# 512 weight columns per product, instead of 256, in the value and Fourier projections of a fused two-block kernel

## The reference

```python
for l in range(DEPTH):                       # DEPTH = 2
    proj = h @ w_in[l]                       # 1024 -> 2048: q, k, v, u of 512 columns each
    a = diff_attention(q, k, v, lam, ...)    # 8 heads, two softmaxes per head, minus each other
    f = fourier_mix(u, w_f[l], b_f[l])       # FFT over features and tokens of u, then a product
    h = layer_norm(ALPHA * h + concat(a, f) @ w_o[l])
    h = layer_norm(ALPHA * h + swiglu(h))
# second block: swiglu, then a mixer whose one input projection holds q, k, v, gates and a
# short convolution (stick-breaking attention, 8 heads), then swiglu
```

## Time and profile before

| | |
|---|---|
| median of 3 runs | 1327.15 us (1324.51 to 1329.25) |
| span of the profiled execution | 1327.0 us |
| PE busy | 1239.0 us, 93% |
| PE weight loads busy | 1183.8 us, 89% |
| DVE busy | 857.9 us, 65% |
| ACT busy | 589.8 us, 44% |
| mean granted clock | 0.964 |

### The profile page before, as it was taken

The page is one execution under the profiler, slowest core; times in us unless marked ns, Lnnn a source line. Parts: engine busy times, 40 slices in busy tenths (PEclk is TensorE's granted clock), DMA queues, the critical chain, the costliest instruction groups (busy, mean ns, idle before and its releaser), DMA issues.

```text
span 1327.0 us, 23836 instructions
## 1 busy us (share of the span) xinstructions
PE 1239.0 (93%) x9572; PEld 1183.8 (89%) x9572; DVE 857.9 (65%) x1077; ACT 589.8 (44%) x693; POOL 14.1 (1%) x30
## 2 busy tenths in 40 slices
PE   4998799999999988999994999999999997999996
PEld 3886699999897687999994999999998997999996
DVE  7674756777857657577778467778458567544445
ACT  5543444333444335344335433444487534444432
POOL 0000000000000000000000000000000000000000
PEclk9999899999899898999996999998999998999998
DMA  7510256677442113577770467773432553455540
GB/s 285 201 64 32 96 191 231 270 276 282 175 149 86 63 64 129 188 284 276 271 275 33 174 224 283 283 274 140 154 133 96 191 188 130 160 190 190 184 164 32
DMA packets 34093, 235.95 MB, mean 178 GB/s; under 512 B 3600, under 2 KB 7200, under 8 KB 7408
## 3 DMA queue, kind: packets, MB, share of 16 engines
q1 hardware_dynamic: 28960, 196.10, 40.2%
q0 software_dynamic: 3584, 38.22, 7.8%
q10 hardware_dynamic: 1488, 0.76, 0.2%
HBM read 234.02 MB, written 1.05 MB: 177 GB/s over the span
## 4 chain that ended last, share of the span: by engine, by line
PE 86%; DVE 6%; ACT 4%; issue 3%; DMA 1%; SPq 0%; DVEq 0%; ACTq 0%
PE bank L335 78%; PE bank L454 2%; ACT w_hi L670 2%; PE bank L434 1%; PE bank L474 1%; DVE rstd L967 1%; PE bank L486 1%; DMA raw<-stream 1%; DVE partial L1011 1%; PE bank L466 1%; DVE w_lo L937 1%; DVE state L960 1%; PE bank L450 0%; DVE state L973 0%; DVE x_lo L979 0%
## 5 line engine op out<-in xcount | busy, mean ns | idle before, releaser
L937 DVE TENSOR_TENSOR w_lo<-raw,w_hi 128x2048 fp32r<-128x2048 f32 x184 | 421.4, 2290 | 240.9 <-ACT w_hi L670 238.3
L335 PE MATMUL bank<-x_hi,w_hi 128*128 128x256 f32 x1888 | 541.3, 287 | 25.3 <-DVE x_lo L979 24.3
L335 PE MATMUL bank<-x_lo,w_hi 128*128 128x256 f32 x1888 | 537.9, 285 | 0.0
L335 PE MATMUL bank<-x_hi,w_lo 128*128 128x256 f32 x1888 | 537.5, 285 | 0.0
L670 ACT ACTIVATE w_hi<-raw 128x2048 fp32r<-128x2048 f32 x184 | 350.2, 1906 | 156.9 <-PE bank L335 154.3
L335 PEld LDWEIGHTS bank<-x_hi,w_hi 128*128 128x128 f32 x1888 | 366.0, 194 | 32.0 <-DVE x_lo L979 15.8
L335 PEld LDWEIGHTS bank<-x_lo,w_hi 128*128 128x128 f32 x1888 | 366.2, 194 | 0.0
L335 PEld LDWEIGHTS bank<-x_hi,w_lo 128*128 128x128 f32 x1888 | 366.0, 194 | 0.0
L335 PE MATMUL bank<-hid_hi,w_lo 128*128 128x256 f32 x704 | 197.9, 281 | 0.0
L335 PE MATMUL bank<-hid_hi,w_hi 128*128 128x256 f32 x704 | 197.3, 280 | 0.0
L335 PE MATMUL bank<-hid_lo,w_hi 128*128 128x256 f32 x704 | 195.8, 278 | 0.0
(11 more groups left out here) (158 smaller groups left out, 1175.7 us busy)
## 6 DMA issues: line engine op xcount, KB each, us to landing
raw<-stream SPq DMA_DIRECT2D x184, 1024.0 KB, 4.8
work<-ada POOLq DMA_DIRECT2D x24, 1536.0 KB, 7.1
state<-xT SPq DMA_DIRECT2D x4, 256.0 KB, 3.6
outT<-state SPq DMA_DIRECT2D x4, 256.0 KB, 2.2
c<-consts SPq DMA_DIRECT2D x1, 960.0 KB, 9.9
wf<-w_f ACTq DMA_DIRECT2D x2, 256.0 KB, 3.1
c<-consts POOLq DMA_DIRECT2D x1, 384.0 KB, 5.6
lp<-layer_params ACTq DMA_DIRECT2D x2, 83.5 KB, 2.5
```

What stands on the lines that cost most here:

```text
L335: last = nc.tensor.matmul(out, stationary, moving, start=start and i == 0, stop=stop and i == 2, skip_group_check=True)
L937: nc.vector.tensor_tensor(w_lo[j % SLOTS][:, :], raw[j % SLOTS][:, :], w_hi[j % SLOTS][:, :].bitcast(F32), ALU.subtract).then_inc(lo_ready, 1)
```

## The change

A chunk of v or u now holds 4 tiles of input features for all 512 output columns, where it held 8 tiles for 256; the stream is repacked on the host and keeps its size and its count of chunks. `token_projection` replaces the natural products: for each tile and each half of the tokens three products that stream 512 columns into a whole bank. Bank 0 gets tokens 0 to 127 and bank 1 the others, and both are complete only when the second of the two chunks is through. So PE's count of natural products goes from 480 to 240, with the same number of streamed columns.

```diff
+            def token_projection(t, j, banks, xh, xl, c, before=lambda k: None):
+                pe.wait_ge(lo_ready, 3 * t + (j + 1))
+                wh, wl = chunk(w_hi, j % SLOTS, 4), chunk(w_lo, j % SLOTS, 4)
+                for i in range(4):
+                    k = 4 * c + i
+                    before(k)
+                    for m in range(2):
+                        cols = slice(m * P, (m + 1) * P)
+                        last = passes(banks[m][:, :], wh[:, i, :], wl[:, i, :], xh[:, k, cols], xl[:, k, cols], True,
+                                      k == 0, k == KT - 1)
+                last.then_inc(chunk_done, 1)
...
-                projection_pair(t, V0, B[0:2], x_hi, x_lo, lambda k: pe.wait_ge(x_ready, 16 * l + (k + 1)),
-                                natural=True)
+                for c in range(2):
+                    token_projection(t, V0 + c, B[0:2], x_hi, x_lo, c, lambda k: pe.wait_ge(x_ready, 16 * l + (k + 1)))
...
                     if s >= 2:
                         transpose_a(s - 2)
-                    if s % 2 == 0:
-                        pe.wait_ge(proj_evac, 8 * l + (j - 1))
-                    projection(t, j, B[j % 2], x_hi, x_lo, ks=range(4 * (s % 2), 4 * (s % 2) + 4),
-                               natural=j in (U0, U1))
+                    if s < 4:
+                        if s % 2 == 0:
+                            pe.wait_ge(proj_evac, 8 * l + (j - 1))
+                        projection(t, j, B[j % 2], x_hi, x_lo, ks=range(4 * (s % 2), 4 * (s % 2) + 4))
+                    elif s % 2 == 0:
+                        if s == 4:
+                            pe.wait_ge(proj_evac, 8 * l + 6)
+                        token_projection(t, j, B[0:2], x_hi, x_lo, j - U0)
...
+                def evacuate_tokens(j, out):
+                    act.wait_ge(chunk_done, 3 * t + (j + 2))
+                    for m in range(2):
+                        nc.scalar.activation(out[:, m, :], B[m][:, :], ACT.Copy).then_inc(proj_evac, 1)
...
                 split(t, 2, first=True)
-                evacuate(V0)
+                split(t, 3)
+                evacuate_tokens(V0, v_s)
+                split(t, 4)
...
-                    if s < 8 and s % 2 == 1:
+                    if s in (1, 3):
                         evacuate(Q1 + s // 2)
+                    elif s == 5:
+                        split(t, U0 + 3)
+                    elif s == 7:
+                        evacuate_tokens(U0, u_s)
+                        split(t, U1 + 3)
...
-            projection_pair(t, 0, B[0:2], x_hi, x_lo, input_tile(6), natural=True)
+            for c in range(2):
+                token_projection(t, c, B[0:2], x_hi, x_lo, c, input_tile(6))
```

More of the change, by code:

```diff
@@ L529, in _ @@
                         pe.wait_ge(consts_landed, 32)
-                    if s == 4:
-                        pe.wait_ge(proj_evac, 8 * l + 6)
                     scores(s)
@@ L754, in evacuate @@
                     act.wait_ge(chunk_done, 3 * t + (j + 1))
[L755 to L762, removed]
+                    half = 0 if j in (Q0, K0) else 1
+                    nc.scalar.activation((qT if j in (Q0, Q1) else kT)[:, 2 * half:2 * half + 2, :],
+                                         B[j % 2][:, :].rearrange("p (m n) -> p m n", m=2), ACT.Copy,
+                                         scale=HD ** -0.5 if j in (Q0, Q1) else 1.0).then_inc(proj_evac, 1)
                     split(t, j + 3)
+                def evacuate_tokens(j, out):
+                    act.wait_ge(chunk_done, 3 * t + (j + 2))
+                    for m in range(2):
+                        nc.scalar.activation(out[:, m, :], B[m][:, :], ACT.Copy).then_inc(proj_evac, 1)
                 def exps(h):
@@ L796, in _ @@
                    .then_inc(wf_landed, 16)
-                for j in (V1, Q0, K0):
+                for j in (Q0, K0):
                     evacuate(j)
@@ L853, in _ @@
                 if j < 2:
-                    out, scale = v_s[:, :, j * S:(j + 1) * S], 1.0
-                elif j % 2 == 0:
+                    if j == 1:
+                        for m in range(2):
+                            nc.scalar.activation(v_s[:, m, :], B[m][:, :], ACT.Copy).then_inc(proj_evac, 1)
+                    split(t, j + 3)
+                    continue
+                if j % 2 == 0:
                     out, scale = qT[:, j - 2:j, :], VD ** -0.5
@@ L1455 @@
         w_in = _tiles(a["w_in"][l], KT, 256)
-        q, k, v, u = w_in[0:2], w_in[2:4], w_in[4:6], w_in[6:8]
+        q, k = w_in[0:2], w_in[2:4]
+        v, u = _tiles(a["w_in"][l][:, 2 * ATT:3 * ATT], 4, ATT), _tiles(a["w_in"][l][:, 3 * ATT:], 4, ATT)
         chunks += [v[0], v[1], q[0], k[0], q[1], k[1], u[0], u[1]]
@@ L1461 @@
     m = _tiles(a["w_mix_in_2"][0], KT, 256)
-    cb, cc, cx, q, k, v, ga, gb = m[0:2], m[2:4], m[4:6], m[6:8], m[8:10], m[10:12], m[12:16], m[16:20]
+    cb, cc, cx, q, k, ga, gb = m[0:2], m[2:4], m[4:6], m[6:8], m[8:10], m[12:16], m[16:20]
+    v = _tiles(a["w_mix_in_2"][0][:, 5 * ATT:6 * ATT], 4, ATT)
     chunks += [v[0], v[1], q[0], k[0], q[1], k[1], *cb, *cc, *cx, *ga, *gb]
```

## The result

Four runs of the changed kernel gave 1343.9 us in the median (1343.48 to 1345.86), four of the kernel before 1326.16 us (1324.51 to 1329.25). The ratio is 1.0135 with a 95% interval of 1.0117 to 1.0152: 18 us slower. The forecast was 1338 us with an upper end of 1344: the side is right and the size too small. The median lies 0.1 us under that end; the ratio on the 1327.15 us that the forecast started from gives 1345.1, 1 us over it.

What follows compares the result with a forecast made beforehand. PE, busy 93% of the span, was taken as the bound, with DVE and ACT close behind in the head stages. Value projections 0.7, bunching 5.8 and clock 4.5 gave +11.0 us on 1327.0: 1338 us, range 1328 to 1344.

Steps and rivals of the forecast that it cites:

- Wide product: On PE at full clock, a product of 512 columns takes 0.2267 us, between bounds of 0.2133 and 0.24.
- Hand-over: From last value product to Q0: 1.15 us start to start, as ACT waits for both banks; 0.72 us more, three times.
- The value side as a whole: Three value projections: 1.5 us saved in products, 2.2 us lost before Q0, net +0.7 us (-0.7 to +2.2).
- Bunching at full clock: Head stages: whole U0 and U1 delay scores of heads 4 and 6; 2.9 us longer a layer, 5.8 in all.
- Clock, first stretch: Head stages, 80.44 to 89.87 in layer 0: the clock falls, costing 1.5 to 4.9 us, middle 3 a layer.
- if it falls: Clock term of the head stages: +4.5 us in sum, between 0 and +8.3 should the clock fall, -1.5 otherwise.
- Clock, what goes away: Layer 1 head stages: the old clock fall, paid at 439.20, is replaced, -1.5 us.
- Clock, second stretch: From 95.31 to past 104 in layer 0: the clock falls, but last scores have 2.5 us of slack; nothing counted.
- A: Head stages: only the bunching counts and the clock falls no more than before, 1332 to 1333.5 us; chance 0.18.
- B: PE alone decides: later scores are caught up by slack, fewer products save 5.4 us, 1324 us; chance 0.1.
- C: Whole kernel: saving and bunching cancel within measurement, 1327 to 1331 us; chance 0.12.
- D: Clock falls in both stretches of a layer, the second also reaching the last head, 1341 to 1345 us; chance 0.1.

Runs made afterwards that it cites:

- 5 full products: Changed kernel plus 5 zero-operand products of 512 columns on all 128 rows in stage 5: 1336.45 us against 1327.35 for the kernel before, ratio 1.0071.
- U halved: Changed kernel with each wide chunk of U0 and U1 cut in two, over stages 4 to 7: 1328.21 us against 1328.74 for the kernel before, ratio 0.9993.
- the narrow bunched one: Kernel before, 256 columns wide, with all of U0 in stage 4 and all of U1 in stage 6: 1344.37 us against 1328.74, ratio 1.0114.
- the one with only U1 cut: Changed kernel with U0 whole in stage 4, U1 cut in two over stages 6 and 7: 1340.84 us against 1327.35 for the kernel before, ratio 1.0105.
- the one with 32 rows: Changed kernel plus 5 zero-operand products on 32 of 128 rows in stage 5: 1344.34 us against 1326.46 for the kernel before, ratio 1.0130.

## Why the prediction fell short

The mechanism and the places were right. The step that failed is the size of one term, what the fallen clock costs in the first stretch; two smaller terms of the clock were off as well and cancel each other.

- Wide product: 0.2267 us estimated, 0.2273 measured.
- Hand-over: 1.15 us estimated, 1.15 measured. The value side as a whole was put at +0.7 us. It is +1.5 in the profile, of which 0.75 is left with the clock evened out, and +2.1 (0.9 to 3.3) when made alone.
- Bunching at full clock: 2.9 us a layer estimated, 2.95 measured (with 5 full products against U halved).
- Clock, first stretch: this is the term that was mis-sized. It was put at 3 us a layer, midway between 1.5 and 4.9; it was 4.7, 75.00 less 70.25 in layer 0, and 4.6 in layer 1. The low bound had the clock fall as the stretch ends, so that only the projection behind it pays. It fell at 86.28, 5.3 us after the stretch had begun at 80.95. All that followed ran at half clock: the products with v, the scores of head 5, the transposes and the first products of U1, until about 96.5. And this fall came every time the stretch was left alone or filled on 32 rows only, in eight layers of eight: the changed kernel, the narrow bunched one, the one with only U1 cut and the one with 32 rows. No run shows a price in the middle between a late and an early fall. (The bounds were also added up wrongly: 2 x 1.5 - 1.5 is 1.5, not 0, at the low end of "if it falls".)
- Clock, what goes away: 1.5 us was taken off for the old fall at 438 in layer 1, none for that at 66.0 in layer 0. In the changed kernel both were gone: -3.1 us, not -1.5. The one at 66 went by chance, as far as the runs show: nothing was changed at that place, and four of the five other kernels with U0 whole have a fall at 66 to 68 us in their profile.
- Clock, second stretch: "I count nothing". Against the last maxima that held, but the first Fourier products then ran at half clock, and the stretch behind the maxima is 1.6 us longer in layer 0. In the timeline of PE:

```profile
113.15 3.62 PE L499 MATMUL bank<-c,work 128*128 128x512 f32 x4
...
117.62 1.94 PE L499 MATMUL bank<-c,work 128*128 128x512 f32 x4
```

  The first four records take 3.62 us and the next four 1.94. In layer 1 before had paid that already (3.66).

Together 2 x 2.95 + 2 x 4.7 - 3.1 + 1.5 = 13.7 us in the heads and behind them, where 10.3 was forecast; 13.6 is what the profiles show. With 1.5 of the value projections, 0.5 before them and -0.3 elsewhere that is 15.3, where 11.0 was forecast. The other 2.5 us up to 18 are in the reference point: the span of before was taken for its time, and that execution was some 2.5 us slower than the median.

The rivals: A (no more falls, 1332 to 1333.5) is refuted by the windows, and the kernel with 5 full products shows it as it would have been, with the second stretch still falling: 9 us slower than before. B fell with DVE's waits before the maxima. C fell with both. The measured time lies in the range of D (1341 to 1345), and the clock did fall in both stretches. But the second fall didn't delay the last head, whose maxima follow DVE's split without a gap at 112.14; it cost its 1.5 us behind it, in one layer out of two. D's time was reached mainly by the first stretch.

## What to carry to other kernels

A wide product that replaces two narrow ones saves about 0.013 us here. The narrow ones that lay between the steps of a latency chain were worth far more, as filler and as what kept the clock up. When a change merges work units, look first at where the units stood in the order, and cut the new ones to the same grain (and signal a bank when it is full, not when its partner is). Where a new stretch is made of the same narrow steps as one in which the clock has fallen, and is twice as long, price a fall in its middle and not at its end, and ask of every old fall whether it stays.

## What the runs showed of the hardware

- A float32r product of 128x512 starts 0.227 us after the last at full clock and 0.427 at the low clock; one of 256 columns 0.120 and 0.213. The part that isn't columns is 0.013 to 0.014 us per product at full clock, for either width, and none is seen at the low clock.
- The clock fell from 2.4 to 1.2 GHz with PE busy 4.00 of 4.00 us, in stretches of scores (32 rows), products with v (64 columns) and transposes. Five products of 512 columns on all 128 rows in such a stretch of 9 us kept it at 2.4 GHz in both layers, although their stationary operand was all zeros, and ten did so too; five on 32 rows did in neither.
- In the changed kernel each of the four falls of the head stages lasted 10.2 us, where each of before lasted 3.4. In the other kernels the falls in the stretches of 9 us lasted 6.8 to 13.7 us.
